# The first matmul phase of a two-block transformer kernel, its loads and its order rebuilt

## What is computed

```python
def rmsnorm(x, g):
    xf = x.astype(f32)
    y = xf * lax.rsqrt(jnp.mean(xf * xf, axis=-1, keepdims=True) + EPS)
    return (y * g.astype(f32)).astype(x.dtype)

def swiglu(x, w_gate, w_up, w_down):
    return (jax.nn.silu(x @ w_gate) * (x @ w_up)) @ w_down

def hybrid_layer(x, norm_ffn1, ffn1_gate, ffn1_up, ffn1_down, norm_mix, w_in, ...):
    x = x + 0.5 * swiglu(rmsnorm(x, norm_ffn1), ffn1_gate, ffn1_up, ffn1_down)
    h = rmsnorm(x, norm_mix)
    ...
```

## Time and profile before

| | us |
|---|---|
| median of 3 runs | 1156.83 (1156.73 to 1156.84) |
| the profiled execution, its own time | 1156.76 |
| its span, first to last instruction | 1155.0 |
| PE busy | 1144.9 (99%) |
| DVE busy | 865.0 (75%) |
| ACT busy | 653.7 (57%) |
| POOL busy | 60.7 (5%) |

### The profile page before, as it was taken

One profiled execution on the slowest core, in us unless ns is written; L12 is line 12 of the kernel. 1 busy time (PEld: TensorE's weight loads), 2 busy tenths in 40 slices (PEclk: granted clock), 3 DMA queues, 4 the chain that ended last, 5 costly groups with the idle time before them and its releaser, 6 DMA issues.

```text
span 1155.0 us, 16192 instructions
## 1 busy us (share of the span) xinstructions
PE 1144.9 (99%) x6258; PEld 964.2 (83%) x6258; DVE 865.0 (75%) x1393; ACT 653.7 (57%) x1096; POOL 60.7 (5%) x77
## 2 busy tenths in 40 slices
PE   8999999999999999999999999999999999999998
PEld 7888888888889888888886788888888887888887
DVE  7788976556667779988688779787787858676754
ACT  7554654466655565555477555555546775555551
POOL 0000000000002000500122100000020001000000
PEclk9999999999999999999999999999999999999999
DMA  9786974755444489998542267878737524667641
GB/s 354 268 297 234 343 279 143 291 188 187 139 170 151 173 318 331 357 338 323 184 151 78 98 251 270 311 288 313 277 145 273 180 106 165 225 230 255 235 148 37
DMA packets 42237, 262.94 MB, mean 228 GB/s; under 512 B 7472, under 2 KB 7856, under 8 KB 12336
## 3 DMA queue, kind: packets, MB, share of 16 engines
q1 hardware_dynamic: 42016, 261.64, 63.2%
q10 hardware_dynamic: 144, 0.26, 0.1%
HBM read 260.79 MB, written 1.10 MB: 227 GB/s over the span
## 4 chain that ended last, share of the span: by engine, by line
PE 91%; DVE 5%; ACT 2%; POOL 1%; issue 1%; POOLq 0%; DVEq 0%; ACTq 0%
PE ps L354 88%; DVE wl L1046 2%; PE ps L958 1%; PE ps L717 1%; PE ps L521 1%; PE ps L1026 0%; DVE xn L1169 0%; PE ps L832 0%; ACT wh L1692 0%; POOL small L2105 0%; DVE x L1081 0%; POOL res L2111 0%; DVE arena L1499 0%; DVE xn L1109 0%; ACT arena L1723 0%
## 5 line engine op out<-in xcount | busy, mean ns | idle before, releaser
L1046 DVE TENSOR_TENSOR wl<-raw,wh 128x1024 fp32r<-128x1024 f32 x374 | 450.6, 1223 | 18.6 <-ACT wh L1692 18.1
L1692 ACT ACTIVATE wh<-raw 128x1024 fp32r<-128x1024 f32 x374 | 388.3, 1052 | 39.1 <-PE ps L354 29.4
L354 PE MATMUL ps<-x,wh 128*128 128x512 f32 x1568 | 393.4, 393 | 0.0
L354 PEld LDWEIGHTS ps<-x,wh 128*128 128x128 f32 x1568 | 285.3, 188 | 56.7 <-issue 2.2
L354 PEld LDWEIGHTS ps<-x,wl 128*128 128x128 f32 x1568 | 213.9, 190 | 15.3
L354 PE MATMUL ps<-x,wl 128*128 128x256 f32 x1568 | 218.5, 282 | 0.0
L354 PE MATMUL ps<-wh,x 128*128 128x512 f32 (+1 forms) x600 | 183.6, 382 | 0.3
L354 PE MATMUL ps<-wh,hh 128*128 128x512 f32 x404 | 160.0, 396 | 0.0
L354 PE MATMUL ps<-wl,hh 128*128 128x512 f32 x404 | 158.0, 391 | 0.0
L354 PE MATMUL ps<-wh,hl 128*128 128x512 f32 x404 | 157.3, 389 | 0.0
L354 PEld LDWEIGHTS ps<-wh,x 128*128 128x128 f32 x600 | 110.5, 188 | 21.9 <-issue 0.7
(11 more groups left out here) (189 smaller groups left out, 861.9 us busy)
## 6 DMA issues: line engine op xcount, KB each, us to landing
raw<-in_stream SPq DMA_DIRECT2D x233, 1024.0 KB, 5.0
arena<-vectors SPq DMA_DIRECT2D x12, 512.0 KB, 6.4
arena<-in_tables SPq DMA_DIRECT2D x7, 576.0 KB, 5.9
raw<-in_stream SPq DMA_DIRECT2D x4, 512.0 KB, 6.1
gain_sb<-in_gains SPq DMA_DIRECT2D x3, 512.0 KB, 7.6
gain_sb<-in_c SPq DMA_DIRECT2D x2, 512.0 KB, 7.1
res<-in_x SPq DMA_DIRECT2D x3, 256.0 KB, 7.0
out_dram<-res SPq DMA_DIRECT2D x3, 256.0 KB, 2.0
```

The costliest lines, as they stand in the source:

```text
L354: return e.matmul(o, a, b, start=start, stop=stop)
L1046: e.tensor_tensor(WL[:, n % NW, :], src, WH[:, n % NW, :].bitcast(F32), ALU.subtract).then_inc(*w_lo.tick(n))
L1692: e.activation(WH[:, m % NW, :], src, ACT.Copy).then_inc(*w_hi.tick(m))
```

## The change

- SP loads all four row halves first (256 KB each), then units 0 and 1 as four column halves of 256 KB with a semaphore each (`half_in`), then units 2 and 3 singly, then as before. The second row half no longer goes through ACT's queue; ACT issues the small `first_gain` load instead.
- ACT squares all four row halves before anything else. Its high parts of units 0 and 1 are made in halves (`first_high_half`), and so are DVE's low parts (`first_low_half`). The eight `first_high` and eight `first_low` steps are spread between the units 0 to 4.
- The scaling of the rows of t = 1 moves from DVE to POOL.
- PE goes through units 0 and 1 in pieces by hand, and from unit 2 on both tiles use a unit before the next unit. The transposes come in four groups of four: before the first piece, after the second, before unit 3 and in the middle of unit 3. In the pieces the order of the three products is high x high, low x high, high x low. The number of matmuls and transposes is the same.
- The transposes of the identity ahead of it are 21 instead of 28.

```diff
@@ the signals
-    first_in = [signal(f"first{i}", 16) for i in range(FIRST)]
+    first_in = signal("first", 16)
+    half_in = [signal(f"half{i}", 16) for i in range(4)]
@@ SP, the first loads
-        e.dma_start(RES[0][0], halves(io["x"][0:P, :])[0]).then_inc(*x_in[0].tick())
-        load_unit(0)
-        e.dma_start(first_gain, io["first_gain"]).then_inc(*first_gain_in.tick())
-        for i in range(1, 3):
-            load_unit(i)
-        for c in range(2):
-            e.dma_start(RES[1][c], halves(io["x"][P:2 * P, :])[c]).then_inc(*x_in[2 + c].tick())
-        load_unit(3)
+        for t in range(2):
+            for c in range(2):
+                e.dma_start(RES[t][c], halves(io["x"][P * t:P * t + P, :])[c]).then_inc(*x_in[2 * t + c].tick())
+        for i in range(4):
+            e.dma_start(halves(RAW[:, 0, i // 2, :])[i % 2], halves(io["stream"][0, :, i // 2, :])[i % 2]).then_inc(
+                *half_in[i].tick())
+        for at in range(2):
+            e.dma_start(RAW[:, 1, at, :], io["stream"][1, :, at, :]).then_inc(*(raw_in[1].tick(1) if at else first_in.tick(units[2])))
@@ PE
+        def first_phase():
+
+            side = x_side(0)
+            got = [take(("tm", "gu0", k)) for k in range(KT)]
+
+            def piece(k, t, c):
+                n, b, cs = got[k], 4 + 2 * t + c, slice(512 * c, 512 * c + 512)
+                xh, xl, hi, lo = side(k, t)
+                there = (n,) if c else ("half", n)
+                if k == 0:
+                    claim(b)
+                pe.wait_ge(*hi)
+                pe.wait_ge(*w_hi.of(*there))
+                mm(e, bank(b), xh, WH[:, n % NW, cs], k == 0, False)
+                pe.wait_ge(*lo)
+                mm(e, bank(b), xl, WH[:, n % NW, cs], False, False)
+                pe.wait_ge(*w_lo.of(*there))
+                i = mm(e, bank(b), xh, WL[:, n % NW, cs], False, False)
+                if (t, c) == (1, 1):
+                    i.then_inc(*formed.tick(("used", n)))
+
+            first_move(0, 0)
+            piece(0, 0, 0)
+            piece(0, 0, 1)
+            first_move(1, 0)
+            piece(1, 0, 0)
+            piece(0, 1, 0)
+            piece(0, 1, 1)
+            piece(1, 0, 1)
+            piece(1, 1, 0)
+            piece(1, 1, 1)
+            for k in range(2, KT):
+                if k == 3:
+                    first_move(0, 1)
+                for t in range(2):
+                    if (k, t) == (3, 1):
+                        first_move(1, 1)
+                    for c in range(2):
+                        token_major(got[k], side, k, t, c, False, k == KT - 1, 4,
...
@@ PE, before the first layer
-        for _ in range(28):
+        for _ in range(21):
             e.transpose(bank(7, P), ident[:], ident[:])
@@ DVE
+        def first_low_half(n, c):
+
+            there = (n,) if c else ("half", n)
+            dv.wait_ge(*w_hi.of(*there))
+            cut = lambda x: halves(x)[c]
+            e.tensor_tensor(cut(WL[:, n, :]), cut(RAW[:, 0, n, :]), cut(WH[:, n, :]).bitcast(F32), ALU.subtract).then_inc(
+                *w_lo.tick(there))
+            split[0] = n + c
@@ ACT
+        def first_high_half(n, c):
+
+            ac.wait_ge(*half_in[2 * n + c].of())
+            e.activation(halves(WH[:, n, :])[c], halves(RAW[:, 0, n, :])[c], ACT.Copy).then_inc(
+                *w_hi.tick((n,) if c else ("half", n)))
+            done[0] = n + c
@@ ACT, the start of the program
-        e.dma_start(RES[0][1], halves(io["x"][0:P, :])[1]).then_inc(*x_in[1].tick())
+        e.dma_start(first_gain, io["first_gain"]).then_inc(*first_gain_in.tick())
@@ POOL, after power(0, 0) and power(0, 1)
+        for c in range(2):
+            po.wait_ge(*x_in[2 + c].of())
+            po.wait_ge(*pooled.of("power", 0, 1))
+            e.tensor_scalar(XN[1][c], RES[1][c], rstd[1][:, 0:1], 32.0, ALU.mult, ALU.mult).then_inc(
+                *pooled.tick(("out", 0, 1, c)))
```

More of the change, by code:

```diff
@@ L558, in move, with first_move @@
                 evicted[b] = [x_lo.of("x", q, t, half)]
-        def first_move(t, turn):
-            for j in range(4):
-                b = next(turn)
+        def first_move(t, half):
+            for j in (2 * half, 2 * half + 1):
+                b = 2 * t + j % 2
                 claim(b)
                 place["first", t, j] = b
-                pe.wait_ge(*vec.of("out", 0, t, j // 2))
+                pe.wait_ge(*(pooled if t else vec).of("out", 0, t, half))
                 for i in range(2):
@@ L592, in ffn @@
             if q == 0:
[L593 to L596, removed]
+                first_phase()
+            else:
+                phase([("tm", "gu" + str(i), k) for k in range(KT)], x_side(q), list(range(KT)), TAIL, 0, "gu" + str(i), turn,
+                      lambda t, c: vec.of("rows", i, t) if c else acted.of("wide", i, t), base=4,
+                      before_last=lambda: move(q, 1, turn))
             h_side = lambda k, t: (HH[:, k % KT, P * t:P * t + P], HL[:, k % KT, P * t:P * t + P],
@@ L1209, in ffn @@
             n = N["tm", "gu" + str(i), 0]
-            low_to(n + TAIL - 1)
             if q:
+                low_to(n + TAIL - 1)
                 x_low(q, 1)
[L1213 to L1216, removed]
+            for k in range(TAIL if q else 0, KT):
                 at(n + k)
@@ L1646, in vector @@
         for c in range(2):
[L1647 to L1650, removed]
+            first_rows(c)
+        mean_square(0, 1)
+        first_low(0, 0)
+        first_low_half(0, 0)
+        first_low_half(0, 1)
+        first_low_half(1, 0)
+        first_low(1, 0)
+        first_low_half(1, 1)
+        first_low(0, 1)
         low_to(2)
-        mean_square(0, 1)
-        for c in range(2):
-            first_rows(1, c)
+        first_low(1, 1)
         low_to(3)
-        for j in range(2, 4):
-            first_low(0, j)
+        first_low(0, 2)
+        first_low(0, 3)
+        low_to(4)
+        first_low(1, 2)
+        first_low(1, 3)
         ffn(0, 0)
@@ L1753, in ffn @@
             n = N["tm", "gu" + str(i), 0]
-            high_to(n + TAIL - 1)
             if q:
+                high_to(n + TAIL - 1)
                 x_high(q, 1)
[L1757 to L1760, removed]
+            for k in range(TAIL if q else 0, KT):
                 at(n + k)
@@ L2066, in stick @@
             boundary(6, n)
[L2070 removed]
+        e.dma_start(first_gain, io["first_gain"]).then_inc(*first_gain_in.tick())
         e.preload_act_table_set("silu_and_others")
[L2072 to L2076 removed]
+        for t in range(2):
+            for c in range(2):
+                square(0, t, c)
+        first_high(0, 0)
+        first_high_half(0, 0)
+        first_high_half(0, 1)
+        first_high_half(1, 0)
+        first_high(1, 0)
+        first_high_half(1, 1)
+        first_high(0, 1)
         high_to(2)
[L2078 to L2079 removed]
+        first_high(1, 1)
         high_to(3)
[L2081 to L2082 removed]
+        first_high(0, 2)
+        first_high(0, 3)
+        high_to(4)
+        first_high(1, 2)
+        first_high(1, 3)
         ffn(0, 0)
```

33 lines of the change are left out of this document (12 added, 21 removed).

## The result

The changed kernel takes **1159.44 us** (median of 18 runs, 1158.00 to 1160.81) where the kernel before takes 1156.86 (18 runs, 1156.73 to 1157.14) beside it: a ratio of 1.0021, 95% interval 1.0015 to 1.0028. It is slower, by 2.6 us. The forecast was 1156.2 and its range ended at 1158.3. The profiled execution took 1159.12, with a span of 1157.4 where before had 1155.0. What also changed is the spread, 2.8 us where there were 0.4.

A forecast was written before the change was run, and what follows sets the result against it. PE was taken to bound the kernel (busy 1144.9 of 1155.0 us), with 2.9 us of early waits to win. 1156.76 - 0.8 (early phase) + 0.2 (`c`) = 1156.2 us; own range 1155.3 to 1156.7, 8 in 10 from 1155.0 to 1158.3.

The forecast's parts named there:

- the sum: Whole program: profiled 1156.76, less 0.8 for the early phase, plus 0.2 for the load of `c`, gives 1156.2 us; chance 0.42.
- term for `c`: Ahead of the multiplied rows: `c`, issued 3 us later, makes PE wait 0.1 to 1.3 us; +0.2 taken.
- with the clock too: `c` late by the whole 3 us plus PE at 1.2 GHz: 1158.6; a fifth of 0.30 covered this or twice the slow matmuls.
- the argument that put the clock aside: Early matmuls: the earlier fall followed 2 us of complete idleness, here no idle stretch exceeds 1.3; clock rival's chance 0.30.
- a fifth of 0.30: Share of the low-clock chance given to the clock falling with `c` late or with twice as many slow matmuls, past 1159.1.
- None is longer than 1.3: PE's idle stretches around the first matmul: each at most 1.3 us, against 2 us before the fall at the program's end.
- +1.1 to +1.6: Rival: PE at 1.2 GHz somewhere in 6 to 14 us adds this to the forecast, giving 1157.5; chance 0.30.
- the 4 and 6 of the earlier trace: Equal transposes counted as started per half microsecond, from 3.1 and 6.6, so 0.21 and 0.11 us apart: PE's two clock levels.
- The start of the transposes: Row transposes hang on the second row half, its square at 4.9; they start near 7.2, -0.2 us (-0.5 to +0.1).
- the walk: Early phase stepped through: PE waits 2.2 us where there were 2.9; with the earlier start, -0.8 us taken.
- A queue that had run dry: Load of `c`: if the queue emptied before group 6, `c` lands at 33.3 and PE waits only 0.1 us.
- The wait for unit 3: PE's wait of 1.2 us at 15.35 for DVE's late low part of unit 3, which the new order removes.

The follow-up runs named there:

- whole loads only: Changed kernel with x loaded as two whole tiles and units 0 and 1 whole, rows of 4 KB, nothing else: 1158.63 us, ratio 1.0015.
- 28 at the start: Changed kernel with 28 instead of 21 identity transposes at the start and nothing in the middle: 1157.65 us, ratio 1.0009.
- transposes added: Changed kernel with 28 identity transposes at the start and 14 more before the first piece: 1157.86 us, ratio 1.0009.
- all whole: Changed kernel with `c` loaded behind the gains, 28 + 14 identity transposes, and x and units 0 and 1 loaded whole: 1156.29 us, ratio 0.9996.
- the mixture: Changed kernel with x of t = 0 in halves, x of t = 1 and units whole, `c` early, 23 + 7 identity transposes: 1159.20 us, ratio 1.0016.

## Why the prediction was wrong

**Two costs that the sum didn't have, taken for alternatives.** The sum had nothing for the clock and +0.2 for `c`. Taken away, the low clock gave back 1.3 to 1.6 us and `c` 1.0 to 1.3; the loads in halves, a third cost that it had at nothing, gave back 0.5 to 0.8. The prediction without its term for `c` says 1156.0, and with all three gone the kernel takes 1156.29. With clock and `c` back (whole loads only) it takes 1158.63, where the rival "with the clock too" has 1158.6, and with the halves 1159.44. So the mechanisms were named, and the steps that failed are the argument that put the clock aside, the +0.2, and the chances: clock and `c` together got a part of a fifth of 0.30, as if each made the other unlikely. They added: -2.6 us with both gone, for -1.6 and -1.3 alone.

Nor did the clock make `c` late. `c` is issued behind groups 6 and 7, these wait for the low parts of units 5 and 7, and these for PE's progress. A slow pace moves all of it, the end of the phase too. The last column is the start of the multiplied rows less the phase's end, less the 2.8 us for which PE has other work:

| profile | clock behind 8 us | `c` issued | landed after | phase ends | issue ahead of the end | PE waits |
|---|---|---|---|---|---|---|
| before | up | 24.13 | 7.5 | 33.83 | 9.7 | 0 |
| changed | low | 28.41 | 7.9 | 34.35 | 5.9 | 1.5 |
| whole loads only | low | 28.54 | 7.4 | 34.48 | 5.9 | 1.0 |
| 28 at the start | up | 27.47 | 7.0 | 33.43 | 6.0 | 0.6 |
| transposes added | up | 28.47 | 7.0 | 34.41 | 5.9 | 0.6 |

```profile
27.47 0.43 SPq L406 DMA_DIRECT2D gain_sb<-in_c  x1
...
33.43 1.98 PE L356 MATMUL ps<-x,wh 128*128 128x512 f32 x8
...
36.84 1.26 PE L518 MATMUL ps<-ident,xn 128*128 128x128 f32 x8 [0.49 <-DVE xn L1269]
```

The rebuilt order brings the issue 3.8 us nearer to the phase's end, with the clock up or down. What differs between its four profiles is the landing, 7.0 to 7.9 us, and whether that has to do with the clock no run shows. In the phase itself the low clock cost 0.9 us (34.35 for 33.43 with 28 transposes, first matmuls at 9.17 and 9.26).

**The argument against the clock.** "None is longer than 1.3" rested on a first matmul at 8.92 and transposes of the rows at 7.24. They came at 9.17 and 6.51, and the gap was 1.96. That isn't all. The version with 28 transposes had a gap of 1.48 and kept its clock, and so did the kernel before with 21 and a gap of 1.84. With whole loads and 21 there were two gaps, 1.4 to 1.6 ahead of the transposes of the rows and 1.17 just ahead of the first matmul, and the clock fell in the second. The profiles also differ in PE's work ahead of the gap: the six in which the clock fell had 21 to 23 transposes at the start, and none of the seven with 28 had a fall. How gap and start weigh against each other the runs don't settle. I read one idle stretch at the end of the program as a limit that a fall needs, and it was only one case. The Trainium skill (TensorE: Matmul & The Clock Gate, "A second HAM failure mode: psum-queue depth-cycling") tells of a kernel whose PE "micro-idles" between groups of matmuls, often enough that the clock goes up and down. The fall at 10.1, in the middle of matmuls, agrees with that in part only, since 1.96 us of idleness stood ahead of it and with whole loads the fall came inside a gap. The estimate of its size, +1.1 to +1.6, was right: 1.3 to 1.6. One reading was wrong without harm: the 4 and 6 of the earlier trace rows are transposes that ran in the half microsecond, not that started in it. The two paces hold, by 21 transposes in 4.74 us and the 14 added ones in 1.69.

**The landing of x.** The start of the transposes was costed as one that hangs on the second half, and came out earlier than forecast (second square at 4.16 for 4.9). The gain vector's small rows didn't hold it up. The first matmul hangs on the fourth half, and of that the walk had no landing time: it took four squares in a row. They have 0.40 and 0.64 of waits between them, 1.6 in another profile. There were rows to bound it by. In the trace of the kernel before x of t = 1 was still on its way at 9 to 10 us (its squares start at 10.84), at rates from 246 to 410 GB/s, and the prediction uses none of them. These are two of its stretches (length, all engines' busy times, then PEclk, DMA share, GB/s):

```profile
9.00:9.50 0.50, 0.48 (x3) 0.17 (x2) 0.50 (x3) 0.50 (x2) 0.00 (x0) 1.00 0.86 246
9.50:10.00 0.50, 0.50 (x3) 0.41 (x4) 0.36 (x2) 0.50 (x2) 0.00 (x0) 1.00 1.06 410
```

**The term of `c`.** +0.2 was taken, between 0.1 and 1.3; 1.0 to 1.3 was measured. The issue was forecast at 27.1 with the phase's end at 33.0, 5.9 us apart, and that distance came out as in the table. "A queue that had run dry" came true and didn't help. In the changed kernel nothing passed from 24 to 26 us:

```profile
24.00:25.00 1.00, 1.00 (x6) 1.00 0.00 0
```

Then groups 6 and 7 were issued at 25.76 and 28.03, the second one 0.4 us ahead of `c`, just as before (23.75 and 24.13). So `c` still stood behind them and landed after 7.0 to 7.9 us (7.5 before). The upper bound of the sum, 1.1 to 1.3, was the answer, and the nearest row said so; I took a value near the other end on a supposition about the queue.

**The gain.** The walk said -0.8 at the next stage, with 33.0. With the clock up it ended at 33.43 (28 transposes) and 33.45 (all whole), so -0.4: the first matmul was 0.3 to 0.5 late. The remaining steps hold. The wait for unit 3 went, ACT stood idle for 3.9 us (3.8 forecast) and this cost PE at most 0.2, POOL's scales took 0.94 each (1.3 taken) and hid, and behind 40 us no more than 0.15 us was lost. On POOL's price the Trainium skill's 0.77 us for 512 elements (GPSIMD Engine Reference, section 3.1) was nearer than my 1.3.

## What to carry to other kernels

When two rivals have different causes, one doesn't make the other unlikely: give the case in which both happen its own chance, and its own time. Here they added, and the time for both, 1158.6, had been worked out and was given next to no weight. For a load that is wanted at a fixed point, compare the distance from its issue to that point before and after (9.7 and 5.9 us here) and take the landing time of the trace; an empty queue helps little when the loads just ahead are issued late with it. Where a rebuild moves the start of PE's work forward but not what it needs next, look at what fills the gap, and take the landing time of every load that the first real instruction stands behind, the last one above all, from a stretch in which loads of that shape pass. Filler work on PE that looks useless at the start of a program is cheap to keep. Here 28 transposes instead of 21, with or without 14 more behind them, were worth 1.3 to 1.8 us, while in the kernel before 21 did as well as 28.

## What the runs showed of the hardware

- The granted clock fell to 1.2 GHz at 10.1 us among early matmuls, or at 8.5 to 9 in a gap ahead of them (whole loads), after 21 to 23 transposes and gaps of 1.2 to 3.3 us. Neither the gap alone (28 transposes and 1.48 us) nor the shorter start alone (21 in the kernel before, 1.84 us) brought it in the profiles. With 28 transposes, and 14 more in the gap or not, it stayed up in every profile.
- The spread between runs has more than one source. With x in column halves the runs of the changed kernel spread over 1.6 to 3.4 us, with whole loads 1.8, with `c` early too 1.2, and with the added transposes as well all but one lie within 0.23 us. In the kernel before a later `c` alone made it 1.5 us instead of 0.5.
- From 4 to 5 us the loads moved 254 and 274 GB/s where x came in rows of 2 KB, in the mixture with rows of 4 KB behind it, and 414 with x in rows of 4 KB; behind 5 us the difference shrinks. The Trainium skill (DMA: Bandwidth & Descriptors, "Specifications") has 512 bytes as the smallest transfer for full rate. Both sizes here are above it, and the cause of the low rate stays open.
- `c`, 512 KB issued 0.4 us behind a group of 1 MB, landed 7.0 to 7.9 us later, also where the queue had been empty from 24 to 26 us.
- POOL scales 128 x 512 numbers in 0.94 us, while loads and PE run beside it.
